# The order in which a matmul takes its 512 weight columns, set by the slot of the ring

## The chip, the core and the metric

The kernel runs on one core of a Trainium2 chip. The metric is the device time of one execution in microseconds (us); the kernel before takes 2096.93 us, the median of three runs (2096.77 to 2097.02). The engines are named as in the profile: PE is TensorE, which multiplies matrices, and PEld its loading of the stationary operand; DVE is VectorE, ACT is ScalarE, POOL is GpSimd, and SP is the queue engine that issues most of the DMAs.

## The reference, cut to what matters

Two layers of a decoder over 256 rows of width 2048, all in float32. Each adds a token mixer and then a dense SwiGLU block to the residual stream, each after an RMS norm:

```
h = x
h = h + stick_breaking_mixer(rmsnorm(h, sb_norm), sb_w_qkv, sb_w_o)     # layer 0, 16 heads
h = h + swiglu_ffn(rmsnorm(h, ffn_norm[0]), ffn_w_gate_up[0], ffn_w_down[0])
h = h + chunked_gmlp_mixer(rmsnorm(h, gm_norm), gm_w_in, gm_v_norm, gm_w_s, gm_b_s, gm_w_o)   # layer 1
h = h + swiglu_ffn(rmsnorm(h, ffn_norm[1]), ffn_w_gate_up[1], ffn_w_down[1])
return rmsnorm(h, final_norm)
```

`swiglu_ffn` is `(silu(gate) * up) @ w_down` with `gate, up = split(h @ w_gate_up)`, and its inner width is 5632. Nearly all of the work is in the products of the 256 rows with the weight matrices: 2048x6144 and 2048x2048 in layer 0's mixer, 2048x4096 and 2048x2048 in layer 1's, and 2048x11264 and 5632x2048 twice.

## The kernel before, in words

**Products in three parts.** A float32 product is made of three matmuls in the format fp32r. Each operand is split into a high part (what the format holds) and a low part (the rest), and high x high, low x high and high x low are added up in PSUM. The activations are the stationary operand (128x128 blocks of xT or of hid, each with a hi and a lo tile), the weights are the moving operand, 512 columns at a time, and a PSUM bank of `acc` takes 128 rows x 512 columns of the result.

**Pieces and the ring.** The weights come in 752 pieces of 256 rows (KP = 2 blocks of 128) and 512 columns, 512 KB each. The ring has RING = 4 slots, and piece p uses slot p % 4 of each of three tiles: SP loads the piece into `raw` (L229), ACT copies it into `w_hi` (L354), which rounds it, and DVE subtracts to make `w_lo` (L662). Both work LEAD = 3 pieces ahead of PE. PE then runs the 12 matmuls of the piece in `piece` (L1081 to L1099): eight with w_hi (two blocks k, two row tiles r, the hi and the lo stationary part), after a wait on hi_ready, and four with w_lo, after a wait on lo_ready. The last one increments `used`, on which ACT waits before it fills the slot again. Every piece goes through `piece` but for the first two (`early_piece`, L1143, whose matmuls stand on L1139) and the last four, which are written out at L1354 to L1370. Each phase starts at a multiple of four pieces, so its pieces take slots 0, 1, 2, 3 in turn.

**Addresses.** Within `w_hi` and `w_lo` a slot is 4096 bytes of each partition and a block k is 2048 of these, so a matmul's moving operand is 2048 bytes that follow each other, and so is its output, one bank of `acc`. The stationary operand of a matmul is 512 bytes. The tile `lead_in` (L107) pads so that the region with hid starts at the same place within 512 bytes as w_hi.

**Order.** The order of all work is written out by hand: each engine has a list of pieces with the rest of its work put between them (norms, transposes, attention, activation functions), and semaphores tie the lists together. PE has short f32 matmuls between pieces in the attention (`scores` L1173, `values` L1193, `turn_prob` L1181), in the transposes (`turn` L1105) and in the gMLP mixer (L1322).

Of the kernel before, what the change touches and what calls it, by code (L numbers as in the profile page):

```python
# [5 lines left out]
def hybrid_trunk(nc, x, sb_norm, sb_w_qkv, sb_w_o, gm_norm, gm_w_in, gm_v_norm, gm_w_s, gm_b_s, gm_w_o,  # L6
# [19 lines left out]
    P = 128  # L26
# [16 lines left out]
    RING = 4  # L43
# [26 lines left out]
    def half(v):  # L70
        return v % 2

    ctx = ExitStack()
    with ctx:
        def sb(name, shape, dt=f32):
            return ctx.enter_context(nc.sbuf_tensor(name, shape, dt))
# [5 lines left out]
        h = sb("h", [P, RT, D])  # L82
# [3 lines left out]
        w_hi = sb("w_hi", [P, RING, KP, CH], f32r)  # L86
        w_lo = sb("w_lo", [P, RING, KP, CH], f32r)
# [6 lines left out]
        stop = sb("stop", [P, 3 * P])  # L94
# [105 lines left out]
        def acc_at(chunk, rt):  # L200

            return acc[:, bass.ds(half(chunk) * (RT * CH) + rt * CH, CH)]
# [6 lines left out]
        def x_turned(k):  # L209

            if k < TC and k % 2 == 1:
                return acc[:, (RT + k // 2) * CH:(RT + k // 2) * CH + S]
            return tp[half(k // TC)][:, k % TC * S:(k % TC + 1) * S]

        def tile(t, k):

            return t[:, bass.ds(k, 1), :].rearrange("p k t -> p (k t)")
# [128 lines left out]
        def _(act):  # L346
# [22 lines left out]
            def x_tiles_gained(ks, seen):  # L369
                act.wait_ge(n_turned[0], seen)  # L370
                for k in ks:
                    nc.scalar.activation(tile(xT_hi, k), x_turned(k), ACT.Copy,
                                         scale=cols[:, k:k + 1]).then_inc(n_hi[0], 1)
# [284 lines left out]
        def _(dve):  # L658
# [19 lines left out]
            def x_tiles_low(ks):  # L678
                for k in ks:
                    dve.wait_ge(n_hi[0], k + 1 if k < TC else k // 2 * 2 + 2)  # L680
                    nc.vector.scalar_tensor_tensor(
                        out=tile(xT_lo, k), in0=x_turned(k),
                        scalar=cols[:, k:k + 1], in1=tile(xT_hi, k).bitcast(f32), op0=ALU.mult,
                        op1=ALU.subtract).then_inc(n_lo[0], 1)
# [395 lines left out]
        def _(pe):  # L1080
            def piece(base, it, per, p, chunk, k0, K, hi, lo, first=False):  # L1081

                pe.wait_ge(hi_ready, base + it * per + p + 1)
                for k in range(KP):
                    kt = k0 + k
                    if first:
                        pe.wait_ge(n_lo[0], kt + 1)
                    for r in range(RT):
                        rs = slice(r * P, (r + 1) * P)
                        for part in (hi, lo):  # L1090
                            nc.tensor.matmul(acc_at(chunk, r), part[:, kt, rs], w_hi[:, p % RING, k],  # L1091
                                             start=(kt == 0 and part is hi), stop=False)
                pe.wait_ge(lo_ready, base + it * per + p + 1)
                for k in range(KP):
                    kt = k0 + k
                    for r in range(RT):
                        last = nc.tensor.matmul(acc_at(chunk, r), hi[:, kt, r * P:(r + 1) * P],  # L1097
                                                w_lo[:, p % RING, k], start=False, stop=(kt == K - 1))
                last.then_inc(used, 1)  # L1099

            def turn(dst, src):
# [19 lines left out]
            def turn_x0(ks, loaded):  # L1121
                pe.wait_ge(loaded, 16)
                for k in ks:
                    for r in range(RT):
                        last = nc.tensor.transpose(x_turned(k)[:, r * P:(r + 1) * P],
                                                   h[:, r, k * P:(k + 1) * P], ident[:, :])
                last.then_inc(n_turned[0], 1)
# [76 lines left out]
            def first_round():  # L1204
                for t, (sec, p) in enumerate(FIRST):
                    if sec == 2 and p == 0:
                        pe.wait_ge(q_out, 1)
                    if t < 2:
                        early_piece(t)
                    else:  # L1210
                        piece(AT_QKV, 0, 3 * PD, t, sec, p * KP, KD, xT_hi, xT_lo, first=sec == 0)
                    if t == 1:
                        turn_x(2)
                    if t == 5:
                        pe.wait_ge(rows_loaded, 4 * 16)
                        turn_rows(tp[0][:, 0:4 * KD], rows, 4 * KD)

            def qkv_round(j):
                for sec in range(3):
                    for p in range(PD):  # L1220
                        t = sec * PD + p
                        if p == 0:

                            pe.wait_ge((k_out, v_out, q_out)[sec], j + (1 if sec == 2 else 0))
                        piece(AT_QKV, j, 3 * PD, t, j * 3 + sec, p * KP, KD, xT_hi, xT_lo)
                        attention(j - 1, t)
# [14 lines left out]
            for s, (c, p) in enumerate(SBO_PAIR):  # L1241
                if p * KP >= (ND - 1) * TC and c == 0:
                    pe.wait_ge(o_lo, p * KP + KP)
                elif s == 0:
                    pe.wait_ge(o_lo, (ND - 1) * HG)
                if p == 0 and c == 1:
                    pe.wait_ge(v_out, ND)
                piece(AT_SBO, 0, 2 * PD, s, c, p * KP, KD, hid_hi, hid_lo)
                for i in range(HG):
                    if s == 6 + 2 * i:  # L1250
                        values(g, i)
                    if s == 4 + 2 * i:
                        turn_prob(g, i)
                for i in range(HG):
                    if s == 2 + 2 * i:
                        scores(g, i)
# [31 lines left out]
            for it in range(ND // 2):  # L1288
                for t in range(2 * PF):
                    p = t % PF  # L1290
# [50 lines left out]
            for it in range(ND // 2):  # L1341
                for t in range(2 * PF if it == 0 else ROWWISE):
                    p = t % PF
# [11 lines left out]
            for r in range(RT):  # L1355
                rs = slice(r * P, (r + 1) * P)
                dst = acc_at(1, r)
                for t in range(ROWWISE, 2 * PF):
                    if r == 0:
                        pe.wait_ge(lo_ready, AT_DOWN[1] + it * (2 * PF) + t + 1)  # L1360
                    for k in range(KP):
                        kt = (t - PF) * KP + k
                        nc.tensor.matmul(dst, hid_hi[:, kt, rs], w_hi[:, t % RING, k], start=False, stop=False)  # L1363
                        nc.tensor.matmul(dst, hid_hi[:, kt, rs], w_lo[:, t % RING, k], start=False, stop=False)  # L1364
                        last = nc.tensor.matmul(dst, hid_lo[:, kt, rs], w_hi[:, t % RING, k], start=False,  # L1365
                                                stop=(kt == KF - 1))
# [32 lines left out]
```

## Time and profile before

| what | value |
|---|---|
| median of 3 runs | 2096.93 us |
| the profiled execution's own time | 2096.52 us |
| its span, first to last instruction | 2094.8 us |
| PE busy | 2085.0 us |
| PEld busy | 1727.0 us |
| DVE busy | 1430.5 us |
| ACT busy | 1013.0 us |
| granted clock, mean | 0.999 |
| HBM, mean over the span | 192 GB/s |

A matmul's recorded duration (390 ns) is longer than the distance from its start to the next one's, since matmuls are pipelined; what counts for the time is that distance, which the timeline and the chain of waits give. Weight loads run beside matmuls.

### The profile page before, as it was taken

Reading aid. Unit: us, or ns where it says so; the run is one execution under the profiler, and the core shown is the slowest. Engines: PE = TensorE matmul, PEld = TensorE weight load, DVE = VectorE, ACT = ScalarE, POOL = GpSimd, SP = SyncE. Lnnn points to the kernel's source line nnn. Section 1 sums busy time; section 2 is a strip of 40 time slices with the busy share of each in tenths; the row PEclk is TensorE's granted clock in tenths of the full one; section 3 lists DMA queues with packets and bytes.
Section 4 is the critical chain, followed back from the end, with each engine's and each line's share of the span. In section 5 each row is a group of like instructions: output and inputs, shape, how many; then the busy total and the mean of one; then the engine's idle time right before and its main releaser. Section 6 shows DMA issues by size and latency. Waiting matters only on the chain.

```text
span 2094.8 us, 27155 instructions
## 1 busy us (share of the span) xinstructions
PE 2085.0 (100%) x9279; PEld 1727.0 (82%) x9279; DVE 1430.5 (68%) x1822; ACT 1013.0 (48%) x1285; POOL 16.5 (1%) x30
## 2 busy tenths in 40 slices
PE   9999999999999999999999999999999999999998
PEld 7888888888888888888888888888888888888887
DVE  7787777867666666665557887877666676664444
ACT  6677765544444444444445444554444444444443
POOL 1000000000000000000000000000000000000000
PEclk9999999999999999999999999999999999999999
DMA  7554555666666666555556565556656666655554
GB/s 272 181 190 154 190 179 171 203 197 193 191 191 197 192 191 193 195 192 192 193 198 207 185 205 185 191 184 202 195 189 194 194 195 191 191 194 197 191 192 150
DMA packets 207419, 402.47 MB, mean 192 GB/s; under 512 B 12336, under 2 KB 13056, under 8 KB 206976
## 3 DMA queue, kind: packets, MB, share of 16 engines
q1 hardware_dynamic: 206496, 398.11, 58.3%
q0 software_dynamic: 688, 3.18, 0.4%
q8 instruction: 36, 0.59, 0.1%
q10 hardware_dynamic: 176, 0.40, 0.1%
q14 instruction: 23, 0.19, 0.0%
HBM read 399.55 MB, written 2.10 MB: 192 GB/s over the span
## 4 chain that ended last, share of the span: by engine, by line
PE 99%; issue 0%; DMA 0%; DVE 0%; SPq 0%; ACT 0%; POOLq 0%; POOL 0%; DVEq 0%
PE acc L1091 65%; PE acc L1097 32%; PE tp L1173 1%; PE tp L1193 0%; PE tp L1322 0%; PE acc L1139 0%; DMA h<-in_x 0%; PE tp L1105 0%; PE acc L1365 0%; PE acc L1364 0%; PE acc L1363 0%; PE tp L1181 0%; DVE h L1060 0%; ACT junk L630 0%; DVE h L1047 0%
## 5 line engine op out<-in xcount | busy, mean ns | idle before, releaser
L662 DVE TENSOR_TENSOR w_lo<-raw,w_hi 128x1024 fp32r<-128x1024 f32 x750 | 916.0, 1224 | 584.2 <-ACT w_hi L354 580.3
L354 ACT ACTIVATE w_hi<-raw 128x1024 fp32r<-128x1024 f32 x750 | 793.0, 1060 | 921.3 <-PE acc L1097 917.2
L1091 PE MATMUL acc<-w_hi,xT 128*128 128x512 f32 x4080 | 1010.3, 390 | 0.0
L1091 PEld LDWEIGHTS acc<-w_hi,xT 128*128 128x128 f32 x4080 | 764.7, 188 | 157.9
L1097 PE MATMUL acc<-w_lo,xT 128*128 128x512 f32 x2040 | 545.3, 389 | 0.0
L1097 PEld LDWEIGHTS acc<-w_lo,xT 128*128 128x128 f32 x2040 | 383.0, 188 | 79.6
L1091 PE MATMUL acc<-w_hi,hid_hi 128*128 128x512 f32 x944 | 368.4, 390 | 0.0
L1091 PE MATMUL acc<-w_hi,hid_lo 128*128 128x512 f32 x944 | 367.3, 389 | 0.0
L1097 PE MATMUL acc<-w_lo,hid_hi 128*128 128x512 f32 x944 | 252.3, 389 | 0.0
L1097 PEld LDWEIGHTS acc<-w_lo,hid_hi 128*128 128x128 f32 x944 | 177.2, 188 | 36.8
L1091 PEld LDWEIGHTS acc<-w_hi,hid_lo 128*128 128x128 f32 x944 | 177.3, 188 | 36.7
L1091 PEld LDWEIGHTS acc<-w_hi,hid_hi 128*128 128x128 f32 x944 | 177.2, 188 | 36.6
L862 DVE STREAM_TRANSPOSE tp<-res 32x256 f32<-32x256 f32 x352 | 160.4, 456 | 7.9
L699 DVE STREAM_TRANSPOSE tp<-res 32x256 f32<-32x256 f32 x224 | 102.1, 456 | 4.5
L432 ACT ACTIVATE probT<-prob_blk 32x96 f32<-32x96 f32 x192 | 50.1, 261 | 29.3 <-DVE prob_blk L767 27.0
L541 ACT ACTIVATE gate<-acc,rstd 128x512 f32<-128x512 f32 x44 | 27.9, 685 | 33.2 <-PE acc L1097 33.2
L852 DVE SCALAR_TENSOR_TENSOR res<-acc,rstd,gate 128x512 f32<-128x512 f32 x44 | 31.0, 747 | 9.8 <-PE acc L1097 9.8
L741 DVE STREAM_TRANSPOSE k_t<-k_s 32x256 f32<-32x256 f32 x64 | 27.9, 435 | 1.2
L741 DVE STREAM_TRANSPOSE q_t<-q_s 32x256 f32<-32x256 f32 x64 | 27.8, 435 | 1.2
L871 DVE TENSOR_TENSOR hid_lo<-tp,hid_hi 128x1024 f32 (+1 forms) x22 | 26.8, 1218 | 0.0
L364 ACT ACTIVATE xT<-tp,cols 128x256 fp32r<-128x256 f32 (+1 forms) x48 | 18.9, 475 | 10.0 <-DVE tp L699 9.9
L753 DVE TENSOR_TENSOR_SCAN left<-keep,stop 128x384 f32<-128x384 f32 x16 | 15.3, 954 | 12.0 <-ACT take L416 12.0
(117 smaller groups left out, 429.0 us busy)
## 6 DMA issues: line engine op xcount, KB each, us to landing
raw<-in_ffn_w_gate_up SPq DMA_DIRECT2D x352, 512.0 KB, 4.5
raw<-in_ffn_w_down SPq DMA_DIRECT2D x176, 512.0 KB, 3.5
raw<-in_sb_w_qkv SPq DMA_DIRECT2D x95, 512.0 KB, 4.3
raw<-in_gm_w_in SPq DMA_DIRECT2D x64, 512.0 KB, 4.2
raw<-in_sb_w_o SPq DMA_DIRECT2D x32, 512.0 KB, 3.9
raw<-in_gm_w_o SPq DMA_DIRECT2D x32, 512.0 KB, 3.7
h<-in_x SPq DMA_DIRECT2D x3, 512.0 KB, 8.7
gain_bc<-in_gm_v_norm POOLq DMA_DIRECT2D x1, 1024.0 KB, 5.8
```

What stands on the lines that cost most here:

```text
L354: nc.scalar.activation(w_hi[:, p % RING], raw[:, p % RING], ACT.Copy).then_inc(hi_ready, 1)
L432: last = nc.scalar.activation(dst[b * Q:(b + 1) * Q, ns, a], src[a * Q:(a + 1) * Q, ns, b], ACT.Copy)
L541: last = nc.scalar.activation(gate[:, r], acc_at(0, r), ACT.Silu, scale=rstd[:, 1 + 2 * layer, r:r + 1])
L662: nc.vector.tensor_tensor(w_lo[:, p % RING], raw[:, p % RING], w_hi[:, p % RING].bitcast(f32), ALU.subtract).then_inc(lo_ready, 1)
L699: last = nc.vector.transpose(tp[0][b * Q:(b + 1) * Q, :].rearrange("p (k r q t) -> p k r q t", k=TC, r=RT, q=4)[:, :, :, a], res[a * Q:(a ...
L741: last = nc.vector.transpose(dst[b * Q:(b + 1) * Q, :, :].rearrange("p k (r q t) -> p k r q t", r=RT, q=4)[:, :, :, a], src[a * Q:(a + 1) ...
L852: last = nc.vector.scalar_tensor_tensor(out=res[:, r], in0=acc_at(1, r), scalar=rstd[:, 1 + 2 * layer, r:r + 1], in1=gate[:, r], op0=ALU.m ...
L862: last = nc.vector.transpose(tp[1][b * Q:(b + 1) * Q, :].rearrange("p (k r q t) -> p k r q t", k=TC, r=RT, q=4)[:, :, :, a], res[a * Q:(a ...
L871: nc.vector.tensor_tensor(hid_lo[:, ks, :], tp[1][:, :].rearrange("p (k t) -> p k t", k=TC), hid_hi[:, ks, :].bitcast(f32), ALU.subtract). ...
L1091: nc.tensor.matmul(acc_at(chunk, r), part[:, kt, rs], w_hi[:, p % RING, k], start=(kt == 0 and part is hi), stop=False)
L1097: last = nc.tensor.matmul(acc_at(chunk, r), hi[:, kt, r * P:(r + 1) * P], w_lo[:, p % RING, k], start=False, stop=(kt == K - 1))
L1173: last = nc.tensor.matmul(dst, qT[:, i, rs], kT[:, i, 0:keys], start=True, stop=True)
```

## The change

A helper `swept` rearranges the 512 columns of an access pattern into (h, c, e): h parts, c steps, runs of e columns. The matmuls of `piece` pass both the moving operand and the PSUM output through it, with parameters set by the slot, so that each column still goes to its own place. Slot 0 takes four sweeps, each over every fourth group of four columns (16 bytes; columns 0-3, 16-19, ..., then 4-7, 20-23, ...). Slot 1 takes two sweeps over every second group of four. Slot 2 takes runs of 128 columns in the order 0, 2, 1, 3. Slot 3 keeps the plain order. The matmuls of L1139 and of L1363 to L1365 don't change, and neither does the order in which the terms of an element are added.

```diff
+        SWEEPS = ((4, 4), (2, 4), (2, 128), (1, 512))
+
+        def swept(columns, slot):
+
+            parts, run = SWEEPS[slot]
+            return columns.rearrange("p (c h e) -> p h c e", h=parts, e=run)
...
                         for part in (hi, lo):
-                            nc.tensor.matmul(acc_at(chunk, r), part[:, kt, rs], w_hi[:, p % RING, k],
+                            nc.tensor.matmul(swept(acc_at(chunk, r), p % RING), part[:, kt, rs],
+                                             swept(w_hi[:, p % RING, k], p % RING),
                                              start=(kt == 0 and part is hi), stop=False)
...
-                        last = nc.tensor.matmul(acc_at(chunk, r), hi[:, kt, r * P:(r + 1) * P],
-                                                w_lo[:, p % RING, k], start=False, stop=(kt == K - 1))
+                        last = nc.tensor.matmul(swept(acc_at(chunk, r), p % RING), hi[:, kt, r * P:(r + 1) * P],
+                                                swept(w_lo[:, p % RING, k], p % RING), start=False, stop=(kt == K - 1))
```

## Rows read from the trace of the kernel before

**Rows 1.** The page: span, busy time by engine, clock by slices, chain of waits.
```profile
span 2094.8 us, 27155 instructions
...
PE 2085.0 (100%) x9279; PEld 1727.0 (82%) x9279; DVE 1430.5 (68%) x1822; ACT 1013.0 (48%) x1285; POOL 16.5 (1%) x30
...
PEclk9999999999999999999999999999999999999999
...
PE 99%; issue 0%; DMA 0%; DVE 0%; SPq 0%; ACT 0%; POOLq 0%; POOL 0%; DVEq 0%
PE acc L1091 65%; PE acc L1097 32%; PE tp L1173 1%; PE tp L1193 0%; PE tp L1322 0%; PE acc L1139 0%; DMA h<-in_x 0%; PE tp L1105 0%; PE acc L1365 0%; PE acc L1364 0%; PE acc L1363 0%; PE tp L1181 0%; DVE h L1060 0%; ACT junk L630 0%; DVE h L1047 0%
```

**Rows 2.** PE's waits: who for whom, total us, times, longest.
```profile
PE acc L1132 <- DVE junk L783: 1.5, 1, 1.5
PE tp L1125 <- DMA h<-in_x: 0.5, 1, 0.5
PE acc L1139 <- ACT xT L372: 0.3, 1, 0.3
```

**Rows 3.** Groups by line and shape, PE: count | busy us, mean ns | idle.
```profile
L1091 PE MATMUL acc<-w_hi,xT 128*128 128x512 f32 x4080 | 1010.3, 390 | 0.0
L1097 PE MATMUL acc<-w_lo,xT 128*128 128x512 f32 x2040 | 545.3, 389 | 0.0
L1091 PE MATMUL acc<-w_hi,hid_hi 128*128 128x512 f32 x944 | 368.4, 390 | 0.0
L1091 PE MATMUL acc<-w_hi,hid_lo 128*128 128x512 f32 x944 | 367.3, 389 | 0.0
L1097 PE MATMUL acc<-w_lo,hid_hi 128*128 128x512 f32 x944 | 252.3, 389 | 0.0
```

**Rows 4.** Timeline of PE, one piece in a quiet stretch: start us, us.
```profile
1001.00 1.07 PE L1097 MATMUL acc<-w_lo,hid_hi 128*128 128x512 f32 x4
...
1003.72 0.39 PE L1097 MATMUL acc<-w_lo,hid_hi 128*128 128x512 f32 x1
```

**Rows 5.** Chain of waits in order of time, from 14 us: start us, us.
```profile
14.72 1.85 PE acc L1091 x8
...
17.49 1.81 PE acc L1091 x8
```

**Rows 6.** Busy time in two stretches: PE, PEld, DVE, ACT, POOL, clock, DMA.
```profile
10.00:30.00 20.00, 20.00 (x97) 16.40 (x97) 18.65 (x30) 17.72 (x36) 0.00 (x0) 1.00 0.89 306
1000.00:1020.00 20.00, 20.00 (x90) 16.57 (x89) 10.48 (x12) 8.19 (x8) 0.00 (x0) 1.00 0.56 190
```

**Rows 7.** Timeline of PE, the two bf16 matmuls after the first transposes.
```profile
5.17 0.38 PE L1132 MATMUL acc<-junk 128*128 128x512 bf16 x1
...
5.39 0.38 PE L1132 MATMUL acc<-junk 128*128 128x512 bf16 x1
```

**Rows 8.** Timeline of PE after attention's short matmuls; ten intervals apart.
```profile
309.88 0.40 PE L1091 MATMUL acc<-w_hi,hid_hi 128*128 128x512 f32 x1
...
312.19 0.39 PE L1091 MATMUL acc<-w_hi,hid_hi 128*128 128x512 f32 x1
```

**Rows 9.** Groups by line and shape, PEld; four more groups of these lines alike.
```profile
L1091 PEld LDWEIGHTS acc<-w_hi,xT 128*128 128x128 f32 x4080 | 764.7, 188 | 157.9
```

**Rows 10.** Groups by line and shape, DVE: three transposes with jumps, one unbroken multiply.
```profile
L862 DVE STREAM_TRANSPOSE tp<-res 32x256 f32<-32x256 f32 x352 | 160.4, 456 | 7.9
...
L741 DVE STREAM_TRANSPOSE k_t<-k_s 32x256 f32<-32x256 f32 x64 | 27.9, 435 | 1.2
...
L934 DVE STREAM_TRANSPOSE wsT<-ws_raw 32x512 f32<-32x512 f32 x16 | 11.2, 702 | 0.5
...
L1050 DVE TENSOR_TENSOR res<-h,gain_bc 128x512 f32<-128x512 f32 x2 | 1.4, 693 | 0.1
```

**Rows 11.** The page: the two splits, and a weight load's median us to landing.
```profile
L662 DVE TENSOR_TENSOR w_lo<-raw,w_hi 128x1024 fp32r<-128x1024 f32 x750 | 916.0, 1224 | 584.2 <-ACT w_hi L354 580.3
L354 ACT ACTIVATE w_hi<-raw 128x1024 fp32r<-128x1024 f32 x750 | 793.0, 1060 | 921.3 <-PE acc L1097 917.2
...
raw<-in_ffn_w_gate_up SPq DMA_DIRECT2D x352, 512.0 KB, 4.5
```

## The prediction

> **What bounds the kernel now.** I read the page from the top. The first lines [rows 1] show TensorE (PE) busy in 2085.0 of 2094.8 us, and the chain that ended last is PE for 99%: L1091 and L1097, the two matmul lines that the change edits, hold 97% of it. A busy PE is no proof by itself, since matmuls are pipelined, so the next look is at what PE waits for: 2.3 us in the whole run, all of it in the first microseconds [rows 2]. PE is fed. [...] So the time is a count of matmuls times the interval from one start to the next, and nothing else of size.
>
> The count: `piece` runs 5968 matmuls of 512 columns at L1091 (4080+944+944) and 2984 at L1097 (2040+944) [rows 3], 8952 in all, 12 to a piece, so 746 pieces. The interval: in a quiet stretch the first L1097 matmul of one piece starts at 1001.00 and that of the next at 1003.72 [rows 4]: 12 matmuls in 2.72 us, 226.7 ns each. 8952 x 0.2267 = 2029 us, 97% of the span. That 226.7 ns is the one number that this change can touch.
>
> [...] And the interval is not rigid: right after the short f32 matmuls of a transpose or of the attention, eight matmuls take 1.85 instead of 1.81 us [rows 5], and ten take 2.31 us (309.88 to 312.19 [rows 8]). That is 231.0 against 226.7 ns: 4.3 ns more for ten matmuls, with the same operands in the same tiles. I read this as two streams that meet in SBUF, the moving operand of one matmul and the 128 stationary columns of the next (PEld, 188 ns each, inside every 227 ns interval [rows 9]), which cost more in one phase against each other than in another. It is a reading, not shown: no row names what PE stalls on inside a matmul.
>
> **The change, part by part.** No instruction is added or removed: the same matmuls, weight loads, waits and increments, with a three-step access pattern for the moving operand and for the PSUM output in three of the four ring slots. The same element is summed in the same order, so nothing else in the kernel has to move. The ring has 188 pieces per slot; less the two early pieces (slots 0 and 1, `early_piece`) and the last four (one of each slot, L1363 to L1365), which are not edited, slots 0 and 1 have 186 pieces and slots 2 and 3 have 187. In matmuls: 2232, 2232, 2244, 2244.
>
> Slot 3 is plain: cost nothing, by construction. Slot 2 takes runs of 128 columns in the order 0 2 1 3. Within a run the addresses rise as before, and a jump comes three times in 512 columns. [...] The nearest rows are DVE's transposes: those that read and write runs of 32 elements with jumps between them take 435 ns for 256 columns and 702 ns for 512 [rows 10], (702-435)/256 = 1.04 ns a column. An unbroken elementwise operation runs at (1224-693)/512 = 1.04 ns a column, from DVE's mean of 1224 ns for 1024 columns [rows 11] and 693 ns for a multiply of 512 [rows 10]. Jumps cost DVE nothing there that one could see, and I take nothing for slot 2. The PSUM side, by the same rows: 456 ns into PSUM with jumps against 435 into SBUF, 21 ns in 256 columns at most.
>
> Slots 0 and 1 take four columns (16 bytes) and then jump over twelve or over four. That is 4464 matmuls, and every ns on one is 4.46 us. [...] Nearest row for the size: the 4.3 ns of the disturbed stretches [rows 5, 8], since it is the same matmul with the two streams out of their usual step. An order that stays with every fourth or every second group of four columns meets the weight load, which walks its 512 bytes in plain order, at another rhythm. In the plain order the stream has fallen into the 226.7 ns step by the next piece (14.72 and 17.49 [rows 5]); with another order for each piece of 12, it has to fall in again and again. I take 4.3 ns for slots 0 and 1: 4464 x 4.3 = 19 us.
>
> What lies beside it: a piece of 2.72 us becomes one of 2.77 us. ACT needs 1.06 us and DVE 1.22 us for the split of a piece, and its load lands 4.5 us after issue [rows 11], with the ring four pieces deep, some 11 us. [...] So all of PE's time goes into the end, one for one, and nothing hides it.
>
> The sum, against the profiled execution: its own time is 2096.52 us, 1.7 over the span of 2094.8 [rows 1]; 2096.5 + 19.2 = 2115.7. The median of the three runs is 0.4 above the profiled one: 2116.
>
> [...]
>
> **Rivals.** (a) No change, 2097 (2093 to 2101). [...] For it: the steady interval is the same for three stationary tiles [rows 4, 5], and DVE's jumps are free [rows 10]. Against it: the disturbed stretches. The case that the new order doesn't reach the chip as written ends here too.
>
> [...]
>
> [...]
>
> **Chances.** My forecast (2116, own range 2102 to 2165, from 1 to 15 ns on slots 0 and 1) 0.35; (a) 0.32; (b) 0.13; (c) 0.20. About 0.2% (4.2 us) is what a measurement of this kernel can tell from no change; it corresponds to 0.94 ns on each matmul of slots 0 and 1. Faster 0.20, same 0.32, slower 0.48. The range runs from 2045, most of (c), to 2170, the upper end of the forecast's own; left out are (b) and the best outcomes of (c), about 0.2.
>
> **What would show it.** The starts of matmuls in a quiet stretch tell it directly, slot by slot, since pieces follow each other in slot order. Right: two pieces in four of 2.74 to 2.85 us, two of 2.72. (a): all at 2.72. [...] Slot 2 at 2.72 would show that three jumps are free; if it is longer too, jumps themselves cost, and not the short runs. The PE waits must stay near 2.3 us, the mean weight load near 188 ns, ACT's 1.06 us and DVE's 1.22 us unchanged; a DVE or ACT split that grew would mean that PE's order disturbs other engines, which I cost at nothing. The forecast is wrong if no slot differs from the plain one, or if the difference sits in the waits instead of in the interval.

## The result, and the profile after

The changed kernel takes 2107.95 us (2107.80 to 2108.02, three runs) against 2096.93: a ratio of 1.0052, interval 1.0038 to 1.0066, so 11 us slower. The forecast was 2116, range 2045 to 2170.

The page of the kernel after, to be read beside [rows 1]: the span grew by 11.3 us, PE's busy time by 11.9, and the clock stands where it stood, 0.999 both times.
```profile
span 2106.1 us, 27155 instructions
...
PE 2096.9 (100%) x9279; PEld 1726.6 (82%) x9279; DVE 1430.8 (68%) x1822; ACT 1012.8 (48%) x1285; POOL 16.5 (1%) x30
...
PEclk9999999999999999999999999999999999999999
...
PE 99%; issue 0%; DVE 0%; ACT 0%; POOLq 0%; POOL 0%; DVEq 0%
```

PE's waits, against [rows 2], in the same columns. One is left, 1.5 us: nothing new is waited for.
```profile
PE acc L1140 <- DVE junk L790: 1.5, 1, 1.5
```

The groups that answer to [rows 9, 11]: weight loads and splits take what they took.
```profile
L1098 PEld LDWEIGHTS acc<-w_hi,xT 128*128 128x128 f32 x4080 | 764.3, 188 | 163.9
...
L669 DVE TENSOR_TENSOR w_lo<-raw,w_hi 128x1024 fp32r<-128x1024 f32 x750 | 916.2, 1224 | 593.7 <-ACT w_hi L361 588.9
L361 ACT ACTIVATE w_hi<-raw 128x1024 fp32r<-128x1024 f32 x750 | 792.7, 1060 | 932.9 <-PE acc L1105 928.8
```

The interval has moved. The chain of waits in order of time (start us, us), of which only the rows with a piece's first eight matmuls stand here; from one row's start to the next is one piece. Counted from the first piece, these are slots 0, 1, 2, 3 and 0.
```profile
1507.84 1.81 PE acc L1098 x8
...
1510.54 1.86 PE acc L1098 x8
...
1513.34 1.81 PE acc L1098 x8
...
1516.06 1.81 PE acc L1098 x8
...
1518.78 1.81 PE acc L1098 x8
```
The pieces take 2.70, 2.80, 2.72 and 2.72 us where each took 2.72 before [rows 4]. Averaged over the starts of all pieces that follow each other without a break: 225.2, 232.9, 226.9 and 226.7 ns a matmul, with 0.1 ns between xT and hid. Against the plain 226.67, slot 0 gives back 2232 x 1.46 ns = 3.3 us, slot 1 costs 2232 x 6.25 = 14.0, slot 2 costs 2244 x 0.2 = 0.5, slot 3 nothing. The sum, 11.2, accounts for the growth of the span, 11.3.

### The profile page after: what moved, and what is told of

It is laid out like the page before. It is cut to its first block, busy times and chain, and to the rows that moved or that the text cites. A ratio compares the mean times of both kernels' runs of the same rounds, so it can differ in the third digit from the quotient of the medians.

```text
span 2106.1 us, 27155 instructions
## 1 busy us (share of the span) xinstructions
PE 2096.9 (100%) x9279; PEld 1726.6 (82%) x9279; DVE 1430.8 (68%) x1822; ACT 1012.8 (48%) x1285; POOL 16.5 (1%) x30
## 4 chain that ended last, share of the span: by engine, by line
PE 99%; issue 0%; DVE 0%; ACT 0%; POOLq 0%; POOL 0%; DVEq 0%
PE acc L1098 65%; PE acc L1105 32%; PE tp L1181 0%; PE tp L1201 0%; PE tp L1330 0%; PE acc L1147 0%; PE acc L1140 0%; PE tp L1113 0%; PE acc L1373 0%; PE acc L1371 0%; PE acc L1372 0%; PE tp L1189 0%; PE tp L1133 0%; DVE h L1067 0%; ACT junk L637 0%
```

## The experiments

Twelve kernels. Theory M was that the moving stream and the next matmul's weight load meet in SBUF, and that the order of the columns sets how often. The rivals: F, a fixed price of a 4-byte matmul; P, the order of the PSUM writes; T and J, prices of changing the order and of a jump. In these experiments a slot's average is read off the starts like those above, and single pieces are shown as rows of the chain of waits. Nine of the twelve ran once; their intervals are compared within a trace, where a slot that nothing touches shows 226.67 ns each time.

### The output's order alone, the input's order alone

```diff
-nc.tensor.matmul(swept(acc_at(chunk, r), p % RING), part..., swept(w_hi[:, p % RING, k], p % RING), ...
+nc.tensor.matmul(swept(acc_at(chunk, r), p % RING), part..., w_hi[:, p % RING, k], ...             # output alone
+nc.tensor.matmul(acc_at(chunk, r), part..., swept(w_hi[:, p % RING, k], p % RING), ...             # input alone
```
The same was done to the matmuls with w_lo.

> The changed kernel with the swept order on the PSUM output alone; the moving operand is read in plain order, so columns land in other places (the output is another one). M: all slots at 226.7 ns, as before the change. P: slot 0 at 225.2 and slot 1 at 232.9, as in the changed kernel.

> The changed kernel with the swept order on the moving operand alone and the PSUM output plain (the output's columns land in other places). With the output alone swept, every interval was 226.7 ns. M (reads in SBUF meet): slots 0 to 3 at 225.2, 232.9, 226.9, 226.7 ns and a span near 2106 us, as in the changed kernel. Rival P2 (the two orders must differ or agree for an effect): intervals unlike both kernels.

Output alone: 2097.50 us, every slot at 226.67. Its rows, of one slot; the other three are alike:
```profile
1506.17 1.81 PE acc L1098 x8
1507.98 0.91 PE acc L1105 x4
```
Input alone: 2107.34 us, and 225.2, 232.9, 226.9, 226.7. Its slots 0 and, begun, 1:
```profile
1507.39 1.81 PE acc L1098 x8
1509.20 0.89 PE acc L1105 x4
1510.10 1.86 PE acc L1098 x8
```
So the whole effect of this change lies in how SBUF is read, and P is out. Runs of four columns cost nothing on the PSUM side, at these two steps (32 and 64 bytes): 226.67 ns in every slot.

### Slot 1 alone put back

```diff
-        SWEEPS = ((4, 4), (2, 4), (2, 128), (1, 512))
+        SWEEPS = ((4, 4), (1, 512), (2, 128), (1, 512))
```


> The changed kernel with slot 1's order alone put back to plain. The trace of the changed kernel puts slot 1 6.25 ns a matmul over plain, 2232 matmuls, 14.0 us, and slot 0 1.46 ns under it, 3.3 us. If the slots add up: 2108.0 - 14.0 = 2094.0, 3 us faster than before. If the loss belonged to orders changing from piece to piece, it would stay above 2100.

2098.17 us (11 executions, 2097.64 to 2098.56) against 2097.12 on the same chip: ratio 1.0004, interval 0.9995 to 1.0013. Most of the loss is gone, but 4 us less of it than the expectation said. The chain shows where they are; slots 0, 1 and 2:
```profile
1500.55 1.81 PE acc L1098 x8
1502.36 0.89 PE acc L1105 x4
1503.25 1.84 PE acc L1098 x8
1505.09 0.91 PE acc L1105 x4
1505.99 1.81 PE acc L1098 x8
1507.81 0.91 PE acc L1105 x4
```
Slot 1 is plain now and yet takes 2.74 us: the first five intervals after the swept piece are 230, 236, 228, 232 and 231 ns, and from the sixth on they are 226.7. These 24 ns a piece, 186 times, are 4.5 us, more than the 3.3 that slot 0 gives back. So putting slot 1 back saves 14.0 - 4.5 = 9.5 us in slot 1, and a change of order at a piece's boundary has a price of its own. Slot 2 keeps its order of runs of 128 columns and takes 226.67 ns here, where it took 226.9 behind slot 1's sweeps: the three jumps are free, and the 0.5 us that I put down to slot 2's order was a boundary price too, 2 to 3 ns on the piece's first matmul. Together that is 10.0 us; the spans of the two kernels differ by 10.1 (2106.1 and 2096.0).

### Slot 0's order in two slots, and in all four

```diff
-        SWEEPS = ((4, 4), (2, 4), (2, 128), (1, 512))
+        SWEEPS = ((4, 4), (1, 512), (4, 4), (1, 512))      # alternating
+        SWEEPS = ((4, 4), (4, 4), (4, 4), (4, 4))          # all four
```


> Slots 0 and 2 in four sweeps over every fourth group, slots 1 and 3 plain. If each swept piece keeps slot 0's 225.2 ns of the changed kernel: 4476 x 1.46 ns = 6.5 us, 2090.5. If the phase in which a piece begins decides (all four slots swept gave 2081.7 in one execution and 2094.1 to 2095.6 in eleven), swept pieces differ from 225.2 and executions scatter.

> All four slots take slot 0's order (four sweeps over every fourth group of four columns). In the changed kernel a slot 0 piece averages 225.2 ns a matmul, and after its first five matmuls the starts repeat 230, 224, 221, 218 ns, 223.3 on average. Theory M (the moving stream and the next weight load meet in SBUF, and the order sets how often): the repeating part holds for whole stretches, so the 8952 matmuls gain between 1.5 ns (13 us, 2084 us) and 3.4 ns (30 us, 2067 us). Rival T (the gain belongs to the change of order from slot 3 to slot 0): without changes of order it is gone, 2097 us. Rival P (the order of the PSUM writes does it): the same as M here.

Alternating: 2098.70 us (ratio 1.0006, 0.9997 to 1.0015). The swept pieces keep 225.2 ns, but each plain one behind them pays the settling again (228.7 on average), which eats up the gain: 2.0 ns lost against 1.46 won. The expectation counted the gain and not the way back. Its other branch isn't borne out either: the eleven executions lie within 1.3 us.

All four: median 2094.82 us against 2097.09, ratio 0.9989 (0.9980 to 0.9998). One execution took 2081.69 us and eleven 2094.1 to 2095.6, while the kernel before stays within 2096.5 to 2097.7. The profile is of the one at 2081.69. Its chain, two pieces near 1001 us, then the piece from 1501.23 and the two behind it:
```profile
1001.72 1.79 PE acc L1098 x8
...
1004.40 1.79 PE acc L1098 x8
...
1501.23 1.81 PE acc L1098 x8
...
1503.93 1.82 PE acc L1098 x8
...
1506.66 1.81 PE acc L1098 x8
...
1509.39 1.81 PE acc L1098 x8
```
A piece of 2.68 us, which is 223.3 ns a matmul, then pieces of 2.70, 2.73 and 2.73. So even in one execution this order has more than one step: half of the pieces that follow each other without a break, all of those from 340 to 1190 us among them, take 223.3, and behind 1500 us the pieces go through seven values from 225.0 to 227.7, which average 226.7, no better than plain. M's forecast of 2067 to 2084 us was met by this one execution and missed by the eleven others, which gained 2 us. An execution that stays mostly in the second pattern would take about what those eleven took; that is a reading, not shown, since no profile of a 2095 us one was taken. What chooses the pattern wasn't found. T, by which the gain would be gone, is out for the 2081.69 us execution; in the rest only the 2 us speak against it. It is the fastest kernel here, by 2 us in nearly all executions.

### The stationary operand moved by 16 and by 32 bytes

```diff
-        hid_hi = at("hid_hi", 0, [P, KF, S], f32r)                    # hid_hi 16 bytes; hid_lo 48, as HB grew by 32
+        hid_hi = at("hid_hi", 0, [P, KF * S + 4], f32r)[:, 4:].rearrange("p (k t) -> p k t", t=S)
-        R0 = nc.lookup_mloc(region).addr                              # 32 bytes
+        R0 = nc.lookup_mloc(region).addr + 32
```


> The changed kernel, with hid_hi and hid_lo moved 16 bytes up against w_hi and w_lo; xT stays where it was. M: where a matmul's stationary operand is hid, the intervals of the four slots (225.2, 232.9, 226.9, 226.7 ns in the changed kernel) change by some ns, slot 3's plain order too; where it is xT they stay. Rival P and rival F (a fixed price of 4-byte matmuls): all intervals stay as they are with hid as with xT, since the PSUM writes and the shapes are the same.

> The changed kernel with the region of hid 32 bytes up against w_hi. With 16 bytes, hid matmuls went to 227.2, 231.6, 232.2, 232.8 ns in slots 0 to 3 and xT matmuls stayed. M with a period of 64 bytes: another set again with hid, slot 3's plain order neither 226.7 nor the mean of the two, and xT unchanged. With a period of 32 bytes: back to 225.2, 232.9, 226.9, 226.7 with hid.

2116.18 and 2118.16 us. The first edit makes room between the tiles as well, so it moves hid_hi by 16 bytes and hid_lo by 48, and not both by 16 as the expectation says. With hid stationary the four slots are at 227.2, 231.6, 232.2 and 232.8 ns with 16 bytes, and at 226.7, 233.3, 233.0 and 233.3 with 32; with xT stationary both kernels have the changed kernel's numbers to 0.05 ns. Two pieces of slot 3, plain order, of the kernel with 16 bytes, first with hid, then with xT:
```profile
1040.46 1.86 PE acc L1098 x8
1042.31 0.94 PE acc L1105 x4
...
1510.14 1.81 PE acc L1098 x8
1511.96 0.91 PE acc L1105 x4
```
Here the strongest evidence stands: in plain order, with the same moving operand and the same output, the stationary operand's address is worth 6.1 ns a matmul. The four matmuls with w_lo take hid_hi alone, which moved by 16 bytes, and they show it too: 0.94 us for four against 0.91. F can't give that. And the shift doesn't add one price to every order: slot 3 rises by 6.1 ns, slot 1 falls by 1.3 (232.9 to 231.6). So the two reads bear on each other. No run moved the moving operand along with the stationary one, so that it is the distance between the two that counts, and not the stationary operand's own address, isn't shown. The expectation left the direction open: the shifts make plain order worse.

### Fewer stationary columns

```diff
+                n = (128, 128, 64, 32)[p % RING] if base in AT_DOWN and 0 < k0 < K - KP else P
-                        rs = slice(r * P, (r + 1) * P)
+                        rs = slice(r * P, r * P + n)
```


> The kernel before (plain order), but in the two down projections the pieces of slot 2 load and use 64 of the 128 stationary columns and those of slot 3 32 (first and last piece of a chunk left whole), so part of the output rows miss terms. M: the excess over 213.3 ns follows the number of stationary columns read: 226.7 ns in slots 0 and 1, 220 in slot 2, 216.7 in slot 3. F: 226.7 in all four.

2101.83 us. The weight loads got shorter, but the intervals got longer. Two groups of loads, then a piece of slot 2 and one of slot 3:
```profile
L1092 PEld LDWEIGHTS acc<-w_hi,hid_hi 128*64 128x64 f32 x156 | 20.9, 134 | 12.9
...
L1092 PEld LDWEIGHTS acc<-w_hi,hid_hi 128*32 128x32 f32 x160 | 17.5, 109 | 18.7
```
```profile
1053.42 1.84 PE acc L1092 x8
1055.27 0.92 PE acc L1098 x4
1056.18 1.85 PE acc L1092 x8
1058.04 0.93 PE acc L1098 x4
```
From one 64-column matmul to the next it is 230.0 ns, from one 32-column matmul to the next 231.7. M had forecast 220 and 216.7, F 226.7 in all four slots: both missed, and M in the form "so many stationary columns read, so many collisions" has fallen. The expectation takes 213.3 ns for the 512 columns themselves; the next kernel gives 214.0. The expectation of the next experiment calls this "left it where it was"; it is 3 and 5 ns worse.

### Fewer moving columns in a matmul

```diff
+                m = (1, 2, 1, 4)[p % RING] if 0 < k0 < K - KP else 1
+                cuts = [slice(i * (CH // m), (i + 1) * (CH // m)) for i in range(m)]
...
+                            for cut in cuts:
+                                nc.tensor.matmul(acc_at(chunk, r)[:, cut], part[:, kt, rs], w_hi[:, p % RING, k, cut],
```


> The kernel before in plain order, but in slot 1 each matmul is two of 256 columns and in slot 3 four of 128 (first and last pieces of a chunk whole), each with its own weight load; the sums are the same. If the excess over the columns' time is a price per matmul: 120 ns a matmul of 256 columns, 2.88 us for a slot 1 piece. If it is a price per column: 113.3 ns and 2.72 us. Fewer stationary columns left it where it was, so a price per stationary column read is not expected. In slot 3 the weight load itself should bound: about 109 ns a matmul, as for the short f32 matmuls, 5.2 us a piece.

2444.51 us. Pieces of 24 matmuls with 256 columns:
```profile
1297.63 1.91 PE acc L1094 x16
1299.54 0.96 PE acc L1101 x8
1300.50 1.84 PE acc L1094 x8
```
2.87 us for 24 is 119.6 ns each (119.7 on average). Against 226.7 with 512 columns, 256 columns more take 107.0 ns, 0.418 ns a column. That makes 214.0 ns for 512, near the 0.22 us from one 512-column bf16 matmul to the next in the kernel before [rows 7], and 12.7 ns on top for each matmul: two halves take 239.4 ns and the whole one 226.7. Of these two sizes, then, the price is one per matmul and not per column. That doesn't tell F from M, since every matmul, short or long, has one whole weight load beside it (15627 of each in this kernel). With 128 columns it is 110.6 ns, near the expected 109; that the weight load is what bounds there isn't shown by itself. The plain 512-column piece behind a 256-column one pays 26 ns in its first matmuls, as after a swept one, and the one behind 128-column matmuls 113 ns.

### Fewer stationary columns under the changed kernel's orders

```diff
+                n = 32 if base in AT_DOWN and 0 < k0 < K - KP else P
```
The other lines are those of the experiment before last, on the changed kernel.

> The changed kernel with 32 of the 128 stationary columns in all slots of the down projections (first and last piece of a chunk whole; rows 32 to 127 of each block miss terms). With the plain order, fewer stationary columns didn't lower the interval (230.0 ns at 64, 231.7 at 32). If slot 1's 6.2 ns over plain come from meeting the weight load's reads, they fall to a quarter or go with a quarter of the columns; if they come from the moving stream's own order, slot 1 stays 6 ns over slot 3 and slot 0 1.5 ns under it.

2110.12 us. From slot 0 on, the rows with the first eight matmuls of five pieces:
```profile
1051.87 1.77 PE acc L1099 x8
...
1054.55 1.85 PE acc L1099 x8
...
1057.32 1.84 PE acc L1099 x8
...
1060.08 1.85 PE acc L1099 x8
...
1062.86 1.79 PE acc L1099 x8
```
The pieces take 2.68, 2.77, 2.76 and 2.78 us. Slot 1's excess over plain order has gone (it is now 0.01 us under slot 3, where it was 0.08 over), and slot 0 is 0.10 us under it instead of 0.02. But most of slot 1's part of that is the plain order getting slower: slot 3 rises from 226.7 to 231.7 ns, as with 32 columns in the experiment before last, while slot 1 falls from 232.9 to 230.4 and slot 0 from 225.2 to about 223.7. So slot 1's loss isn't a fixed surcharge of its order, which is what the expectation asked, and the width of the weight load bears on every order, in different directions. That the loss itself shrinks with the columns read isn't shown: of its 6 ns above 226.7 only 2.5 went with three quarters of the columns. Slot 0's gain wasn't expected to grow.

### Other orders, and runs shorter than four columns

```diff
+        SWEEPS = ((8, 4), (16, 4), (2, 8), (4, 8))         # other orders
+        SWEEPS = ((2, 2), (8, 2), (1, 512), (1, 512))      # short runs
```


> Four other orders: slot 0 eight sweeps over every eighth group of four columns, slot 1 sixteen over every sixteenth, slot 2 two sweeps of runs of eight columns, slot 3 four sweeps of runs of eight. M with a period of four groups (64 bytes): slots 0 and 1 stay in one class of addresses as the old slot 0 did, near 225 ns; slots 2 and 3 alternate between two classes, near 230. Rival J (the number of jumps sets the price): 127 jumps in slots 0 and 1, 63 in slots 2 and 3, so slots 2 and 3 are nearer to 226.7 than slots 0 and 1.

> Runs of two columns (8 bytes): slot 0 two sweeps over every second pair, slot 1 eight sweeps over every eighth pair, slots 2 and 3 plain. Theory L (SBUF is read in groups of four columns, so half of each group read is thrown away): slots 0 and 1 cost far more than a few ns, up to double, 427 ns. Rival J (a price per jump, 255 of them against 127): twice the earlier differences, 3 to 12 ns, slot 0 below 240 ns.

In both kernels the moving operand and the PSUM output take the same order, as in the changed kernel. The output alone was tried only with runs of four columns at steps of 32 and 64 bytes and with runs of 128, so for what follows the side that costs isn't told apart.

Other orders: 2272.30 us. Slots 2, 3, 0 and 1 in turn, first rows of each piece:
```profile
1501.52 1.87 PE acc L1098 x8
...
1504.32 1.84 PE acc L1098 x8
...
1507.08 1.97 PE acc L1098 x8
...
1510.04 2.21 PE acc L1098 x8
...
1513.35 0.71 PE acc L1098 x3
```
Pieces of 2.80, 2.76, 2.96 and 3.31 us: 234.1 and 229.8 ns for runs of eight, 246.2 for every eighth group of four, 275.4 for every sixteenth. The period of 64 bytes that I gave M is wrong. J's sign came true (slots 2 and 3 are nearer to 226.7 than slots 0 and 1), but J fails all the same: every fourth, eighth and sixteenth group have the same 127 jumps and take 225, 246 and 275 ns. The length of the step matters, and not in one direction: for groups of four a step of 32 bytes takes 232.9, 64 takes 225.2 and more takes longer; for runs of eight a step of 64 bytes takes more than one of 128, though some of that is the settling behind slot 1.

Short runs: 3074.14 us. A piece of slot 0, then one of slot 1:
```profile
2214.74 3.62 PE acc L1098 x8
2218.36 1.81 PE acc L1105 x4
2220.17 3.50 PE acc L1098 x8
2223.67 1.73 PE acc L1105 x4
```
5.43 and 5.22 us, 451 and 435 ns a matmul on average, where J had at most 240 for slot 0. Twice 226.7 is 453. L has the size right, "up to double": with runs of two columns, the matmul takes 1.9 to 2.0 times as long as in plain order. Whether SBUF reads cost that, as L has it, or PSUM writes in runs of two, isn't shown; no kernel had the output alone in runs of two.

## Why the prediction was right, point by point

It was right on what bounds the kernel and on the direction, and in part by luck: the 11 us are a gain of 3.3 and a loss of 14.0, and the forecast had two equal losses.

**What bounds.** Right. No wait grew, the clock didn't move (0.999), PE holds 99% of the chain, and the 11 us are all in the interval between starts.

**Slots 2 and 3.** Right: slot 3 is untouched, and three jumps cost nothing, as slot 2's 226.67 ns behind a plain slot 1 shows; its 0.2 ns in the changed kernel, 0.5 us in all, belong to the boundary with slot 1. What rested on DVE's rows, that jumps are free, holds for this slot, but DVE's 128-byte runs said nothing of short runs at long steps: every sixteenth group of four costs 49 ns.

**Slots 0 and 1.** The direction of their sum was right and the size too high: I gave both 4.3 ns, 19 us. They measured -1.46 and +6.25, 2.4 on average, 10.7 us. The mis-sized term is this one price for two orders, taken from the disturbed stretches [rows 5, 8], and it stood for the wrong thing: slot 0 has the opposite sign, and slot 1 doesn't "fall in again and again" but has a slower step of its own, intervals of 232.5 and 234.1 ns in turn through the piece. That the average came near is luck. The sign that I gave for being right, two pieces in four of 2.74 to 2.85 us, was met by one, 2.80; slot 0's 2.70 lies under the plain 2.72. Falling in again exists, as the kernel with slot 1 put back shows, but it is paid by the plain piece behind a swept one, 24 ns, and its intervals of 236, 228, 232 and 231 ns also stand in the kernel before, from 310.80 us on, behind the attention's short matmuls [rows 8]. So the nearest row had priced the way back to plain order, which the changed kernel hardly pays: slot 2 takes over from slot 1 for 2 to 3 ns.

**Rival (a)** fails with the trace: slots 0 and 1 differ from 226.7 ns. The chances name two more outcomes. **(b),** that each jump costs, is out for this change: three jumps in slot 2 and the output's order cost nothing, 226.67 ns, and of slots 0 and 1, with 127 jumps each, slot 0 is faster than plain. **(c),** faster, has the sign of slot 0, which gains 1.46 ns a matmul, 3.3 us, and fails with slot 1: the two slots together average 229.1 ns. The lower end of the range, 2045, rests on the author's estimate of how much of the 226.7 ns a new order could give back, about 12 ns in each matmul of slots 0 and 1. No run shows that term; the runs showed 1.46 ns in slot 0 here, and 3.4 in half of the pieces of the execution of 2081.69 us.

**The mechanism.** That the two operands' reads of SBUF bear on each other is shown: the input's order alone has the effect, the stationary operand's address changes it, for slots 1 and 3 in opposite directions, and so does the width of the weight load. That the excess, 12.7 ns by the matmuls of 256 and 512 columns, is a count of collisions in proportion to the stationary columns is refuted: the interval grows when fewer columns are read, from 226.7 to 230.0 and 231.7 ns. That it comes once a matmul fits a fixed price and a meeting with the one weight load alike. What the 12.7 ns are, and why a step of 64 bytes is better than 32, 128 or 256, stays open.

## What to carry to other kernels

Where PE never waits, the time is the interval between matmul starts: read it from the timeline or the chain, slot by slot, before and after, since the busy share (100% both times) and mean durations (390 against 391 ns) don't show that one slot in four has become 3% slower. In this kernel the stationary operand's address was worth up to 3% of a matmul and the access order from -0.6% to +3% in the change and 21% at the longest step, so keep the order plain and the addresses as they measured best unless a measurement says otherwise, and don't take runs of two columns (8 bytes), which doubled the time (435 and 451 against 226.7 ns). A trial of several orders in the slots of one ring gives all their intervals in one profile, but count what each does to the slot behind it.

## What was not expected of the hardware

- A shift of the stationary tiles (hid_hi by 16 bytes, hid_lo by 48) took plain matmuls from 226.7 to 232.8 ns, and one of 32 bytes to 233.3.
- Two matmuls of 256 columns take 12.7 ns more than one of 512 (239.4 against 226.7), which leaves a plain fp32r matmul 12.7 ns over its columns at 0.418 ns each; with 64 or 32 stationary columns it gets slower, 230.0 and 231.7 ns.
- Behind sweeps over every fourth group, five plain matmuls take 228 to 236 ns before the steady 226.7; behind 256-column matmuls it is much the same, behind sweeps over every second group one takes 229, and behind runs of two columns nine take 224 to 246.
- Taking every fourth, eighth or sixteenth group of four columns: 225.2, 246.2, 275.4 ns. Runs of two columns: 435 and 451 ns. For all but the first, whether reading or writing costs isn't shown.
- One kernel with nothing but a repeated order had two times, 2081.7 us once and about 2094.8 eleven times.
